# Neighbourhood attention by pairs of heads: scores of both heads back to back, value products alternating between column halves

## The reference, cut to what matters

```python
def context_attention(q, k, v):                 # 256 queries, 256 keys
    s = jnp.einsum('bqhd,bkhd->bhqk', q, k) * (q.shape[-1] ** -0.5)
    p = jax.nn.softmax(s.astype(F32), axis=-1).astype(v.dtype)
    o = jnp.einsum('bhqk,bkhd->bqhd', p, v)
...
def neighbourhood_attention(q, k, v, k_ctx, v_ctx, rpb):   # 256 queries, 256 latent + 256 context keys
        ...
        s_loc = jnp.einsum('bhqd,bhrqwd->bhqrw', qr, kwin) + bias
        s_ctx = jnp.einsum('bhqd,bhcd->bhqc', qr, kc)
        logits = jnp.concatenate([s_loc.reshape(bsz, nh, GRID_W, n_loc), s_ctx], -1).astype(F32)
        p = jax.nn.softmax(logits, axis=-1).astype(v.dtype)
        ...
        return (jnp.einsum('bhqrw,bhrqwd->bhqd', p_loc, vwin)
                + jnp.einsum('bhqc,bhcd->bhqd', p[..., n_loc:], vc))
```

## Time and profile before

| | us |
|---|---|
| median of 3 runs | 2040.75 (2039.01 to 2041.18) |
| the profiled execution, its own time | 2040.45 |
| its span in the trace | 2038.7 |
| PE (TensorE matmul) busy | 1950.0 (96%) |
| PEld (TensorE weight load) busy | 1535.7 |
| DVE (VectorE) busy | 1267.0 (62%) |
| ACT (ScalarE) busy | 645.4 (32%) |
| POOL (GpSimd) busy | 290.4 (14%) |

### The profile page before, as it was taken

How to read it: one execution, slowest core, us unless ns; L and a number is a source line. 1 busy time by engine, 2 the same in 40 slices (tenths; PEclk the granted TensorE clock), 3 DMA queues, 4 the chain that set the end, 5 groups by cost and what they waited for, 6 DMA issues and landing times.

```text
span 2038.7 us, 24301 instructions
## 1 busy us (share of the span) xinstructions
PE 1950.0 (96%) x9246; PEld 1535.7 (75%) x9246; DVE 1267.0 (62%) x2231; ACT 645.4 (32%) x1093; POOL 290.4 (14%) x318
## 2 busy tenths in 40 slices
PE   6999999999999989899999999999999899989997
PEld 6888878885554454688887888888778867779997
DVE  7677776753872663677678447774677535465454
ACT  2322242323342431422224233222432332324452
POOL 0000001240000002500000122000034535130003
PEclk9999999998997999899999999999999999989999
DMA  8354536313350001245544223553234555214442
GB/s 359 123 203 169 206 139 167 128 54 124 135 217 0 1 0 42 104 170 204 203 165 167 96 114 140 207 206 123 103 115 174 208 193 189 83 42 166 178 168 108
DMA packets 43959, 290.12 MB, mean 142 GB/s; under 512 B 13916, under 2 KB 19676, under 8 KB 27232
## 3 DMA queue, kind: packets, MB, share of 16 engines
q1 hardware_dynamic: 34336, 270.08, 35.2%
q10 hardware_dynamic: 9536, 18.88, 2.4%
HBM read 272.16 MB, written 16.78 MB: 142 GB/s over the span
## 4 chain that ended last, share of the span: by engine, by line
PE 85%; DVE 7%; ACT 3%; DMA 2%; issue 1%; POOL 1%; SPq 0%; ACTq 0%; POOLq 0%; DVEq 0%
PE bank L606 13%; PE bank L611 12%; PE bank L608 12%; PE bank L663 7%; PE bank L669 6%; PE bank L672 6%; PE bank L800 4%; PE bank L797 3%; PE bank L784 3%; PE bank L981 2%; PE bank L737 2%; PE bank L890 1%; PE bank L727 1%; DMA slot<-in_down_dram 1%; PE bank L978 1%; PE bank L936 1%
## 5 line engine op out<-in xcount | busy, mean ns | idle before, releaser
L1701 DVE CUSTOM_DVE_ANT_0 L<-slot 128x1024 f32<-128x1024 f32 x272 | 337.7, 1241 | 72.1 <-DMA slot<-in_ada_dram 65.0
L1165 ACT ACTIVATE w_hi<-slot 128x1024 fp32r<-128x1024 f32 x176 | 186.2, 1060 | 572.7 <-PE bank L611 559.1
L1758 DVE TENSOR_TENSOR w_lo<-slot,w_hi 128x1024 fp32r<-128x1024 f32 x176 | 217.3, 1237 | 218.0 <-ACT w_hi L1165 212.1
L606 PE MATMUL bank<-m_hi,w_hi 128*128 128x512 f32 (+1 forms) x1344 | 296.6, 363 | 3.2 <-ACT w_hi L1165 3.2
L608 PE MATMUL bank<-m_lo,w_hi 128*128 128x512 f32 (+1 forms) x1344 | 296.1, 363 | 0.0
L611 PE MATMUL bank<-m_hi,w_lo 128*128 128x512 f32 (+1 forms) x1344 | 296.1, 362 | 0.0
L606 PEld LDWEIGHTS bank<-m_hi,w_hi 128*128 128x128 f32 x1344 | 232.3, 189 | 43.1 <-ACT w_hi L1165 4.0
L608 PEld LDWEIGHTS bank<-m_lo,w_hi 128*128 128x128 f32 x1344 | 232.5, 189 | 39.3
L611 PEld LDWEIGHTS bank<-m_hi,w_lo 128*128 128x128 f32 x1344 | 232.5, 189 | 39.3
L1917 DVE TENSOR_TENSOR down_lo<-slot,down_hi 128x1408 fp32r<-128x1408 f32 x64 | 108.6, 1710 | 129.2 <-ACT down_hi L1215 128.9
L669 PE MATMUL bank<-g_lo,down_hi 128*128 128x512 f32 (+1 forms) x770 | 156.8, 352 | 0.0
(11 more groups left out here) (345 smaller groups left out, 2658.7 us busy)
## 6 DMA issues: line engine op xcount, KB each, us to landing
slot<-in_gateup_dram SPq DMA_DIRECT2D x44, 2048.0 KB, 7.5
slot<-in_ada_dram SPq DMA_DIRECT2D x34, 2048.0 KB, 7.5
slot<-in_down_dram SPq DMA_DIRECT2D x32, 1408.0 KB, 5.9
slot<-in_ev_in_dram SPq DMA_DIRECT2D x4, 2048.0 KB, 9.7
slot<-in_od_in_dram SPq DMA_DIRECT2D x4, 2048.0 KB, 10.1
R<-s_ops SPq DMA_DIRECT2D x16, 512.0 KB, 5.8
s_tables<-slot ACTq DMA_DIRECT2D x8, 768.0 KB, 3.3
R<-s_tables SPq DMA_DIRECT2D x8, 768.0 KB, 6.1
```

Source lines behind the costliest of these rows:

```text
L606: nc.tensor.matmul(bank[j][:, c0:T], w_hi[:, off, c, :], m_hi[:, c, c0:T], start=(c == 0), stop=False)
L1165: nc.scalar.activation(w_hi[:, off, :, :].rearrange("p a b -> p (a b)"), slots[b][:, (2 * (f % 2) + off) * D:(2 * (f % 2) + off + 1) * D], ...
L1701: ins = nc.vector.tensor_tensor_reduce(out=junk, in0=slots[k][:, t * D:(t + 1) * D], in1=csilu[s_], scale=1.0, scalar=0.0, op0=ALU.mult, o ...
L1758: nc.vector.tensor_tensor(w_lo[b][:, t, :, :].rearrange("p a b -> p (a b)"), slots[b][:, t * D:(t + 1) * D], w_hi[:, off, :, :].bitcast(F3 ...
```

## The change

The units of a group are ordered so that the two heads of the same queries are neighbours, and all steps work on **pairs** of units (16 pairs):

- TensorE issues the scores of a pair back to back, one on rows 0 to 63 and one on rows 64 to 127, two pairs ahead, into four banks (0, 1, 7, 6). They wait for both exponentials of the pair two before (`na_exp_done`), no longer for the reciprocal. The second pair also waits for ScalarE's reading of bank 6.
- VectorE: both maxima of pair p + 1, one reciprocal for both units of pair p, both scalings. The maxima of a pair wait for all transposes of the pair two before, where a unit waited for those of the unit three before. There are four `probs` buffers.
- ScalarE: both exponentials of pair p + 1, then both copies of the transposes of pair p.
- TensorE does the value products of a group in one go (`weigh`), after the transposes of the first pair of the next group; matmuls of head 0 (columns 0 to 63 of the array) and head 1 (columns 64 to 127) alternate. `attention_out` of a group moves back accordingly.

Every matmul, transpose and elementwise operation is still there with the same shape, except that 32 reciprocals of one column become 16 of two.

```diff
-        score_banks = [banks[0], banks[1], banks[7]]
-        probs = [L[:, 0:T], L[:, T:2 * T], R[:, 12288:12288 + T]]
-        probsT = view(L, 2 * T, 2, 4, 2 * P)
+        score_banks = [banks[0], banks[1], banks[7], banks[6]]
+        probs = [L[:, 0:T], L[:, T:2 * T], R[:, 12288:12288 + T], R[:, 5120:5120 + T]]
+        def probsT(st, hh):
+            if st == 0:
+                return view(L, 2 * T + 512 * hh, 2, 2 * P)
+            return view(R, 4096, 4, 2 * P) if hh else view(L, 4 * T, 4, 2 * P)
...
-        UNITS = [(hp, st, hh, qt) for hp in range(4) for st in range(2) for hh in range(2) for qt in range(2)]
+        UNITS = [(hp, st, hh, qt) for hp in range(4) for st in range(2) for qt in range(2) for hh in range(2)]
+        NA_PAIRS = len(UNITS) // 2
...
+                def scores(p):
+                    if p == 0:
+                        pe.wait_ge(sem("even_proj_read"), 24)
+                    if p == 1:
+                        pe.wait_ge(sem("even_acol_ready"), 2)
+                    if p >= 2:
+                        pe.wait_ge(sem("na_exp_done"), 2 * p - 2)
+                    for u in (2 * p, 2 * p + 1):
...
+                        nc.tensor.matmul(score_banks[u % 4][:, 0:keys], na_q[r0:r0 + NA_DIM, hp, q0:q0 + P],
+                                         na_k[r0:r0 + NA_DIM, hp, 0:keys], start=True, stop=True).then_inc(sem("na_scores_done"), 1)
+
+                def weigh(group):
+                    hp, st = group // 2, group % 2
                     tiles = 2 if st == 0 else 4
-                    pe.wait_ge(sem("na_probs_ready"), u + 1)
...
+                    pe.wait_ge(sem("na_pT_ready"), 4 * group + 4)
+                    if group >= 2:
+                        pe.wait_ge(sem("even_y0"), group - 1)
                     for kt in range(tiles):
+                        for hh in range(2):
                             last = nc.tensor.matmul(banks[4 + group % 2][NA_DIM * hh:NA_DIM * (hh + 1), 0:CTX],
                                                     na_v[:, kt, (2 * hp + hh) * NA_DIM:(2 * hp + hh + 1) * NA_DIM],
+                                                    probsT(st, hh)[:, kt, :], start=(kt == 0), stop=(kt == tiles - 1))
+                            if kt == tiles - 1:
+                                last.then_inc(sem("na_out_done"), 1)
+
+                scores(0)
+                scores(1)
+                for p in range(NA_PAIRS):
+                    if p + 2 < NA_PAIRS:
+                        scores(p + 2)
+                    for u in (2 * p, 2 * p + 1):
+                        tiles = 2 if UNITS[u][1] == 0 else 4
+                        pe.wait_ge(sem("na_probs_ready"), u + 1)
+                        if p:
+                            pe.wait_ge(sem("na_pT_ready"), u - 1)
+                        for kt in range(tiles):
+                            last = nc.tensor.transpose(banks[2 + u % 2][:, kt * P:(kt + 1) * P], probs[u % 4][:, kt * P:(kt + 1) * P], ident[:, :])
+                        last.then_inc(sem("na_pT_done"), 1)
+                    if p and p % 2 == 0:
+                        weigh(p // 2 - 1)
+                weigh(NA_PAIRS // 2 - 1)
...
 # VectorE
+                def maxima(p):
+                    if p >= 2:
+                        dve.wait_ge(sem("na_pT_done"), 2 * p - 2)
+                    for u in (2 * p, 2 * p + 1):
...
+                maxima(0)
+                for p in range(NA_PAIRS):
+                    if p + 1 < NA_PAIRS:
+                        maxima(p + 1)
+                    a = 2 * (p % 2)
+                    dve.wait_ge(sem("na_exp_done"), 2 * p + 2)
+                    link(nc.vector.reciprocal(col[:, 8 + a:10 + a], col[:, 4 + a:6 + a]))
+                    for u in (2 * p, 2 * p + 1):
...
+                    if p >= 3 and p % 2:
+                        attention_out(p // 2 - 1)
+                attention_out(NA_PAIRS // 2 - 1)
```

More of the change, by code:

```diff
@@ L872, in even @@
-                for u in range(3):
-                    scores(u)
-                for u, (hp, st, hh, qt) in enumerate(UNITS):
+                    if p == 1:
[3 more added lines that the diff above has]
+                    for u in (2 * p, 2 * p + 1):
+                        hp, st, hh, qt = UNITS[u]
+                        r0 = NA_DIM * hh
+                        q0 = STREAMS[st][0] + qt * P
+                        keys = CTX if st == 0 else T
+                        nc.tensor.matmul(score_banks[u % 4][:, 0:keys], na_q[r0:r0 + NA_DIM, hp, q0:q0 + P],
+                                         na_k[r0:r0 + NA_DIM, hp, 0:keys], start=True, stop=True).then_inc(sem("na_scores_done"), 1)
@@ L1445, in even, with exps @@
-                exps(0)
[L1446 to L1454, removed]
+                def exps(p):
+                    for u in (2 * p, 2 * p + 1):
+                        st = UNITS[u][1]
+                        keys = CTX if st == 0 else T
+                        act.wait_ge(sem("na_max_ready"), u + 1)
+                        src = score_banks[u % 4][:, 0:keys] if st == 0 else probs[u % 4][:, :]
+                        nc.scalar.activation(probs[u % 4][:, 0:keys], src, ACT.Exp, bias=col[:, u % 4:u % 4 + 1],
+                                             accum_out=col[:, 4 + u % 4:5 + u % 4]).then_inc(sem("na_exp_done"), 1)
@@ new lines, in turned_probs @@
+                def turned_probs(p):
+                    for u in (2 * p, 2 * p + 1):
+                        hp, st, hh, qt = UNITS[u]
+                        tiles = 2 if st == 0 else 4
+                        act.wait_ge(sem("na_pT_done"), u + 1)
+                        if p >= 4 and qt == 0:
+                            act.wait_ge(sem("na_out_done"), 2 * (p // 2) - 2)
+                        nc.scalar.activation(probsT(st, hh)[:, :, qt * P:(qt + 1) * P],
+                                             banks[2 + hh][:, 0:tiles * P].rearrange("p (a n) -> p a n", n=P), ACT.Copy).then_inc(sem("na_pT_ready"), 1)
@@ L1457, in even @@
+                exps(0)
+                for p in range(NA_PAIRS):
+                    if p + 1 < NA_PAIRS:
+                        exps(p + 1)
+                    turned_probs(p)
                 slot_done[3] += 1
@@ L2153, in even @@
                 dve.wait_ge(sem("na_bias_masked"), 8)
[L2155 to L2166, removed]
@@ L2168, in even @@
-                maxima(0)
[L2169 to L2179, removed]
@@ L2180, in even @@
-                attention_out(7)
+                def maxima(p):
+                    if p >= 2:
+                        dve.wait_ge(sem("na_pT_done"), 2 * p - 2)
+                    for u in (2 * p, 2 * p + 1):
+                        hp, st, hh, qt = UNITS[u]
+                        dve.wait_ge(sem("na_scores_done"), u + 1)
+                        neg = col[:, u % 4:u % 4 + 1]
+                        if st == 0:
+                            nc.vector.tensor_reduce(neg, score_banks[u % 4][:, 0:CTX], AX.X, ALU.max, negate=True).then_inc(sem("na_max_ready"), 1)
+                        else:
+                            nc.vector.tensor_copy(probs[u % 4][:, 0:CTX], score_banks[u % 4][:, 0:CTX])
+                            link(nc.vector.tensor_tensor(probs[u % 4][:, CTX:T], score_banks[u % 4][:, CTX:T], na_bias[:, qt, 2 * hp + hh, :], ALU.add))
+                            nc.vector.tensor_reduce(neg, probs[u % 4][:, :], AX.X, ALU.max, negate=True).then_inc(sem("na_max_ready"), 1)
@@ new lines, in even @@
+                maxima(0)
+                for p in range(NA_PAIRS):
+                    if p + 1 < NA_PAIRS:
+                        maxima(p + 1)
+                    a = 2 * (p % 2)
+                    dve.wait_ge(sem("na_exp_done"), 2 * p + 2)
+                    link(nc.vector.reciprocal(col[:, 8 + a:10 + a], col[:, 4 + a:6 + a]))
+                    for u in (2 * p, 2 * p + 1):
+                        keys = CTX if UNITS[u][1] == 0 else T
+                        nc.vector.tensor_scalar(probs[u % 4][:, 0:keys], probs[u % 4][:, 0:keys], col[:, 8 + u % 4:9 + u % 4], None,
+                                                ALU.mult).then_inc(sem("na_probs_ready"), 1)
+                    if p >= 3 and p % 2:
+                        attention_out(p // 2 - 1)
```

14 lines of the change are left out of this document (1 added, 13 removed).

## The result

| | us |
|---|---|
| before, median of 4 runs | 2039.88 (2037.14 to 2041.18) |
| after, median of 4 runs | 2025.11 (2023.96 to 2026.11) |
| ratio, 95% interval | 0.9925 (0.9913 to 0.9936) |
| the profiled execution after, its own time and span | 2024.13, 2022.4 |

The kernel is 15 us faster; 2026.5 was forecast. In the profiled executions the span is 16.3 us shorter. The attention took 85.0 us (631.0 to 716.0) and now takes 69.4 (629.7 to 699.1).

A forecast was written before the change was run, and what follows sets the result against it. TensorE bounds the old attention (16.6 of 17.85 us per head pair), then VectorE with its waits. First head pair 16.7, two of 16.0, the last 14 and the end reach 702: 14 us less, 2026.5 us, range 2015 to 2038.

The forecast's parts named there:

- Sum: Whole attention: ends near 702 instead of 715.96, 14 us less, giving a median of 2026.5 us.
- A pair of scores at the price of one, both heads' value products at the price of one: TensorE in the attention: neighbours in array halves run side by side, saving 3.3 us (scores) and 2.95 (products) per head pair.
- Rival 1: Value products: column halves do not run side by side; 16.0 us per head pair, about 2034 us in all; chance 0.13.
- What bounds it then: Attention after the change, upper clock: VectorE with its waits bounds; four intervals together 13.4 us per head pair against 17.85.
- A: Interval between ends of transposes, first to second context pair: 4.0 us at the upper clock, TensorE's work hidden.
- B: Interval from second context to first latent pair's transposes: 4.6 us at the upper clock, TensorE waiting over 2.5 us.
- C: Interval from first to second latent pair's transposes: 2.75 us at the upper clock, decided by TensorE.
- D: Interval from second latent pair's transposes to the next head pair's first: 2.05 us at the upper clock.
- Lower level: Attention at 1.2 GHz: TensorE decides all intervals but B; 6.65, 5.4, 5.0 and 3.05, together 20.1 us per head pair.
- Which clock: TensorE's clock in the attention: first fall stays, return about 651, then one fall per head pair in B, 2.6 us each.
- Fill and end: Attention's start and finish: first transposes end about 636.4; last copy 0.64, product 1.94, copy 0.44, ending at 702.
- Nothing to take it back: Behind the attention: the mLSTM starts on TensorE and VectorE alone, no DMA runs, so all that follows moves forward.

The follow-up runs named there:

- six buffers: The change with six row buffers (`probs`) instead of four, so maxima wait for the transposes of the pair three before: 2018.57 us, 0.9887.
- filled kernels: Kernels with matmuls of no use added where TensorE waits; the change with two per head pair ahead of the first latent transposes: 2016.95 us, 0.9881.
- both kernels filled: The kernel before with two matmuls of no use behind its first three scores (2033.3 us, 0.9962), and the change filled twice (2018.25 us, 0.9890).
- filled twice: The change with matmuls of no use ahead of each head pair's first latent transposes and two more behind the first scores: 2018.25 us, 0.9890.
- B filled: The change with two matmuls of no use per head pair ahead of the first latent pair's transposes: 2016.95 us, 0.9881.

## Why the prediction was right

**Sum.** 14 us were forecast for the attention; 15.6 came in the profiled executions, 15 in the medians. By its steps:

- *A pair of scores at the price of one, both heads' value products at the price of one*: right: a pair of latent scores takes 1.13 us where one took 1.12, and sixteen product instructions 1.95 where eight took 1.94. The rule of the Trainium skill (TensorE: Matmul & The Clock Gate, Part 3, The mechanism) that weight loads overlap running matmuls only for another row group is not borne out here: column halves load side by side, 0.01 us apart, at 651.39 and 651.40, while the matmuls of 651.12 and 651.13 (0.43 us each) still run. Rival 1 fell with it, though its price was right once the halves were really taken apart (16.1 us per head pair against 16.0 forecast).
- *What bounds it then*: A 4.0, B 4.6, C 2.75, D 2.05 were forecast; 4.1, 4.7, 2.7 and 2.0 to 2.1 measured with the clock held, 13.6 against 13.4. VectorE's wait for the transposes is a real term: six buffers take it away.
- *Lower level*: B 5.4 and C 5.0 were forecast; 5.5 (first head pair, all of it low) and 4.6 (second head pair, almost all low) measured.
- *Which clock*: back at 651 was forecast, 648 measured; one fall per head pair in B and a return in C, as forecast (falls at 658.2, 675.2, 688.9). Two head pairs were forecast at 16.0 each; from the end of one first context pair's transposes to the next head pair's they are 16.3 and 15.1. A fall was priced at 0.35 us in B and 2.25 in C; it cost 0.8 in B and 0.8 to 2.0 in C, 1.6 to 2.8 in all. The filled kernels show that the wait in B is the cause.
- *Fill and end*: the first transposes were forecast to end at 636.4 and ended at 635.2; that is the attention's earlier start, since from its start to there are 5.5 us, and 5.4 were forecast. The attention ended 3 us before the forecast 702: 1.3 are that start, and the rest is 0.7 us less in the first head pair (16.0 against 16.7), 0.7 less in the two behind it together (31.3 against 32) and 0.6 less in the last (13.4 against 14).
- *Nothing to take it back*: nearly so. The mLSTM starts 16.9 us earlier and is through 16.3 earlier. Its own falls of the clock moved (two of 3.4 us now, one of 6.8 before), though its code is the same in both kernels.
- *Luck*: that the medians are 1.4 us from the forecast is closer than it could be known. The pattern of the clock differs between two executions of the same kernel (34.1 and 27.3 us low in the attention).

**What was wrong in it.** The prediction set the gain against 17.85 us as if all of it were the two halves. With the clock held, rows give 1.05 us per head pair and columns 2.5, together 3.5 of 17.85 - 13.6 = 4.3; that the two add was not run with both fully apart, so the remaining 0.7 for the looser order is a difference, not a measurement. And it took the low clock of the kernel before for a thing that only a denser order would end; two matmuls of no use at the start do that too, for 10 us of the attention. That does not take these 10 us off the change, which had a low clock of its own to pay for (69.4 us against 61.2 filled): with both kernels filled, the attention goes from 75.3 to 61.2 us, 14 us that are the change's own. The prediction also had the first fall stay because "waiting for the first units" stays. The fall did stay, but it came at 630.87, 0.02 us after the end of the first scores, with hardly any of that wait ahead of it, and in the change filled twice it came at 632.0 with none. What the wait does is keep the clock down: with B filled it is low for 13.6 us at the start without the second filling and for 3.4 with it. Last, in the head pair of the earlier trace rows the chain leaves TensorE three times, not twice (a copy by ScalarE at 694.13 as well), for 4.7 of 17.85 us; TensorE's own sum of 16.6 us still makes it the bound.

## What to carry to other kernels

Matmuls that use half of the rows or half of the columns are worth putting next to each other: here two heads cost what one did. Look at what bounds the stage once they do; here it was the buffer that the other engine waits for, and two more of them took 8 us more off, beside the 15 of the change. And where TensorE waits in a stage of short matmuls, read the granted clock by stretch before anything else: here a wait of 1.3 us at the start cost the kernel before 10 us of its attention, beside the 14 to 16 that the whole reordering gave. Matmuls of no use in the wait may pay, if they don't hold back the first useful one.

## What the runs showed of the hardware that was not expected

- TensorE begins a matmul of the other column half while three older instructions of the first half still stand before it: 653.14, beside head 0's fifth of eight. With four per head the two heads ran fully side by side, written in either order (1.09 us).
- Two float32 weight loads and two matmuls in different column halves start 0.01 us apart in each of the pairs, and none is slower than alone (matmuls of 0.38 us, the first of a product 0.43, in both kernels).
- A TensorE that is busy by the records for 23.90 of 23.90 us still stayed at 1.2 GHz for all of them; with the wait of 1.3 us ahead of it filled, the same work ran at 2.4 GHz up to 698.8.
- Clock falls in the mLSTM, in code common to all these kernels, come at other places from trace to trace, and are good for some 3 us: the span behind the attention of the run with value products head by head is 4.6 us longer than after the change, 3.0 of it in the mLSTM, with 17 us of low clock there against 6.8.
